# Moving the ring of low weight parts by 64 bytes in SBUF

## What is computed

```
first_block, per layer:   h = x @ w_in;  three attention branches;  gates * (branch @ w_branch)
                          x = layernorm(ALPHA*x + merged @ w_out)
                          x = layernorm(ALPHA*x + square(relu(x @ mlp_w1)) @ mlp_w2)
second_block, per layer:  u = rmsnorm(h);  u @ w_in_2;  SSD, HGRN2 and mLSTM branches
                          h += merged @ w_out_2
                          h += (silu(conv(u @ w_up)) * v) @ w_down
                          h += (p @ w_ple) * sigmoid(h @ w_ple_gate)
out = rmsnorm(h)
```

## Time and profile before

| | |
|---|---|
| time, median of 3 runs | 2486.16 us (2485.28 to 2489.66) |
| the profiled execution's own time | 2493.97 us |
| its span, first to last instruction | 2492.2 us |
| mean granted TensorE clock | 0.994 |
| PE busy, PEld busy | 98%, 90% of the span |
| DVE, ACT, POOL busy | 72%, 58%, 12% of the span |

### The profile page before, as it was taken

The page is one execution under the profiler, slowest core; times in us unless marked ns, Lnnn a source line. Parts: engine busy times, 40 slices in busy tenths (PEclk is TensorE's granted clock), DMA queues, the critical chain, the costliest instruction groups (busy, mean ns, idle before and its releaser), DMA issues.

```text
span 2492.2 us, 43110 instructions
## 1 busy us (share of the span) xinstructions
PE 2440.8 (98%) x17744; PEld 2232.4 (90%) x17744; DVE 1786.6 (72%) x2889; ACT 1452.0 (58%) x2130; POOL 291.6 (12%) x222
## 2 busy tenths in 40 slices
PE   8999999999999999899999999999999999999998
PEld 8888999988889899799999799998898999899996
DVE  4567675565576755669867887885599768887875
ACT  5547555445466455467665655664667656656654
POOL 0000002000000000002222720000012207500000
PEclk9999999999999999899999999999999999999999
DMA  7554476555544565555566655566554567645663
GB/s 248 157 145 118 154 247 193 186 185 168 140 125 142 173 201 186 168 158 144 145 178 186 194 153 192 187 192 197 149 161 135 162 191 197 184 148 190 189 210 127
DMA packets 358920, 430.50 MB, mean 173 GB/s; under 512 B 20616, under 2 KB 286310, under 8 KB 358468
## 3 DMA queue, kind: packets, MB, share of 16 engines
q1 hardware_dynamic: 341312, 401.72, 53.1%
q10 hardware_dynamic: 14340, 14.93, 2.7%
q0 software_dynamic: 3072, 11.10, 1.5%
HBM read 424.44 MB, written 3.24 MB: 172 GB/s over the span
## 4 chain that ended last, share of the span: by engine, by line
PE 87%; DVE 9%; ACT 2%; issue 1%; DMA 1%; ACTq 0%; POOL 0%; POOLq 0%; DVEq 0%
PE ps L112 85%; PE ps L115 2%; DVE wlo L121 2%; DVE sE L121 1%; DVE hgA L148 1%; DVE hgQF L121 0%; DVE hgQB L121 0%; ACT lnv L118 0%; DVE hgkf L121 0%; DVE hgkb L121 0%; DMA kT<-in_diff_lambda 0%; DVE sbc L130 0%; DVE sE L124 0%; DMA memN<-in_mem 0%; DVE hgTf L121 0%
## 5 line engine op out<-in xcount | busy, mean ns | idle before, releaser
L121 DVE TENSOR_TENSOR wlo<-wring,whi 128x1024 fp32r<-128x1024 f32 (+1 forms) x768 | 919.2, 1217 | 252.7 <-ACT whi L118 252.1
L118 ACT ACTIVATE whi<-wring 128x1024 fp32r<-128x1024 f32 (+1 forms) x768 | 803.5, 1054 | 427.9 <-PE ps L112 415.8
L112 PE MATMUL ps<-uT,whi 128*128 128x256 f32 x4640 | 817.8, 280 | 6.1 <-DVE wlo L121 4.5
L112 PEld LDWEIGHTS ps<-uT,whi 128*128 128x128 f32 x4640 | 705.8, 188 | 16.4 <-DVE wlo L121 7.5
L112 PE MATMUL ps<-uT,wlo 128*128 128x256 f32 x2320 | 645.4, 278 | 0.0
L112 PEld LDWEIGHTS ps<-uT,wlo 128*128 128x128 f32 x2320 | 436.1, 188 | 0.0
L112 PE MATMUL ps<-xT,whi 128*128 128x256 f32 x2112 | 381.0, 284 | 2.9 <-DVE xT L121 1.7
L112 PEld LDWEIGHTS ps<-xT,whi 128*128 128x128 f32 x2112 | 323.4, 188 | 9.7 <-issue 5.6
L112 PE MATMUL ps<-xT,wlo 128*128 128x256 f32 x1056 | 296.4, 281 | 0.0
L112 PE MATMUL ps<-whi,hid 128*128 128x512 f32 x864 | 270.4, 392 | 0.0
L112 PEld LDWEIGHTS ps<-xT,wlo 128*128 128x128 f32 x1056 | 199.4, 189 | 0.3
(11 more groups left out here) (400 smaller groups left out, 3576.9 us busy)
## 6 DMA issues: line engine op xcount, KB each, us to landing
wring<-in_w_in SPq DMA_DIRECT2D x346, 512.0 KB, 4.2
wring<-in_mlp_w SPq DMA_DIRECT2D x128, 512.0 KB, 4.4
wring<-in_w_up SPq DMA_DIRECT2D x88, 512.0 KB, 4.5
wring<-in_w_down SPq DMA_DIRECT2D x44, 512.0 KB, 4.5
wring<-in_w_branch SPq DMA_DIRECT2D x32, 512.0 KB, 3.4
wring<-in_w_out SPq DMA_DIRECT2D x32, 512.0 KB, 4.6
wring<-in_mem_w_kv SPq DMA_DIRECT2D x16, 512.0 KB, 5.9
wring<-in_w_br_hg SPq DMA_DIRECT2D x16, 512.0 KB, 4.6
```

The source lines that it names most:

```text
L112: return self.e.matmul(*p, **k) if self.e else Nothing()
L118: return self.e.activation(*p, **k) if self.e else Nothing()
L121: return self.e.tensor_tensor(*p, **k) if self.e else Nothing()
```

## The change

The tensor of the low parts gets 32 floats (128 bytes) more, and the ring is the stretch of it that begins 16 floats (64 bytes) in. So all operands from `wlo` begin at 64 modulo 128. `wring` and `whi` stay where they are. Everything allocated behind `wlo` moves by 128 bytes, so its place modulo 128 stays, the arena's too; the arena's size, rounded down to 64 floats, stays 36672 floats, and so does every offset in it.

```
-    K.whi, K.wlo = sb("whi", NS * WN, F32R), sb("wlo", NS * WN, F32R)
+    K.whi, K.wlo = sb("whi", NS * WN, F32R), sb("wlo", NS * WN + 32, F32R)[:, 16:16 + NS * WN]
```

## The result

The changed kernel takes 2532.84 us (median of 4 runs, 2525.15 to 2533.62); the kernel before, run beside it, 2486.8 us (2485.28 to 2489.66). The ratio is 1.0168, 95% interval 1.0146 to 1.0189: 1.7% slower. The forecast was 2500 us with a range up to 2520, so the direction held and the size did not: 42 us by the ratio (0.0168 x 2486.8), 46 us by the two medians, where 14 were forecast. The profiled execution took 2533.62 us, its span 2531.8 us. Beside the traced execution of before, itself a slow one of its kernel (2493.97 us where the median is 2486.8), the span grew by 2531.8 - 2492.2 = 39.6 us.

A forecast was written before the change was run, and what follows sets the result against it. TensorE's matmul pace was taken to bound the kernel. Features +13.6 us and tokens +2.1 us, times 0.9, gave +14 us on the 2486.2 us median: 2500 us, range 2464 to 2520.

The forecast's parts named there:

- What bounds the kernel: TensorE, busy 98% of the span, sets the time; features triples have two steady speeds, 13.5 ns apart.
- Its signs: Features' wlo groups at 279 ns or more, none at 276, no triple at 0.340 us; uneven steps; token groups leaving 389.
- VectorE, 0: The subtraction's output shifted by 64 bytes costs 1 ns, 0.8 us over 768, mostly beside TensorE's work; taken as 0.
- A wait or an engine that becomes late: No wait is added; VectorE, if slowed, would be late on the 9% of the chain that is DVE.
- The features' term: One odd load in three costs 1950 quick features triples 7 ns each: +13.6 us, bounds -26.6 and +26.3.
- The tokens' terms: Token triples with stationary operand at 0: 304 x 7 ns = +2.1 us; about 780 at 64: 0, bounds -6.8 and +8.8.
- The upper end of the range: Range top 2520 us, above 2517 us for all features slow and tokens at their bound, less a tenth.
- The tenth taken off: Features before a wait on wlo or a transposition gain nothing, so the summed TensorE terms were multiplied by 0.9.
- The move of everything else by 128 bytes, 0: Everything behind wlo moves by 128 bytes but keeps its place modulo 128; cost taken as 0.
- third rival: With a 256-byte pattern, the arena's move changes activations' distance to whi; all features slow, +26.3, about 2514 us; chance 8%.
- First rival, likeness helps: Load and stream at the same place modulo 128 run faster on TensorE: 2477 us, down to 2453; chance 36%.
- Second, places don't matter: Features' two speeds come from how work falls after each break, not place: 2486 us, give or take 4; chance 16%.

The follow-up runs named there:

- both64: Kernel before with both rings (high and low parts) beginning at 64 modulo 128, arena where it was: 2535.61 us, ratio 1.0173.
- x0all: Kernel before with the whole arena beginning 64 bytes further on, rings unmoved, most activations at distance 0 from both rings: 2539.25 us, ratio 1.0214.
- lo128: Kernel before with the low ring alone moved by 128 bytes modulo 256, constants allocated between the rings: 2484.99 us, ratio 0.9976.
- pad128: Kernel before with only what lies behind the low ring moved by 128 bytes, the ring staying at 0 modulo 128: 2524.13 us, ratio 1.013.
- w256: Kernel before with a 256-byte buffer allocated ahead of the rings instead of behind, moving both rings by 256 bytes, arena unmoved: 2483.32 us, ratio 1.0.
- (192, 64): Placement of lo128 and best: activations start 192 bytes past the high ring and 64 past the low ring, modulo 256; ratios 0.9976 and 0.9977.
- (192, 192): Placement of the kernel before and w256: most activations start 192 bytes past both rings, modulo 256; ratios 1 and 1.0.
- best: lo128 with three buffers (first-block merged, second-block hid, hT) 64 bytes lower: 2483.01 us, ratio 0.9977 to the kernel before.
- x160: Kernel before with the rings beginning 32 bytes further on, arena unmoved: 2532.24 us, ratio 1.0185.
- x224: Kernel before with the arena beginning 32 bytes further on, rings unmoved: 2535.01 us, ratio 1.0197.
- pad_lo128: lo128 with `wlo` 32 floats longer, moving everything behind the rings by 128 bytes: 2506.34 us, ratio 1.0074 to the kernel before.
- before_xl64: Kernel before with the low halves of uT alone 64 bytes further on, rings untouched: 2507.11 us, ratio 1.0078.

## Why the prediction was wrong

**What bounds the kernel** was read rightly: TensorE's pace, with two steady speeds of features at 340 and 353.5 ns, and the place of operands modulo some power of two behind it. The 40 us between the traces are of that kind. Its signs came true as well: the wlo groups of features have 283 and 282 ns, 16 quick triples are left, the steps are uneven, and the token groups at 389 rose.

**VectorE, 0:** right, 1222 ns. **A wait or an engine that becomes late:** none.

**The features' term is the step that failed.** The prediction said that a triple with one odd step "cannot settle in the same way", and the quick speed did go, but then it took for it "the nearest measured cost of an operand at the other place, 7 ns a triple". If the quick speed can't be reached, the quick triples fall all the way to the slow speed, which the same profile had at 13.5 ns. Measured: 16 quick triples left, and a mean of 353.2 where it was 346.0. The term was 13.6 us and came out at 28 us by paces; the bound of +26.3 stood in the text, and was the value that the argument called for. The count was a little off as well: by starts 56% of triples were quick before, about 2200 and not 1950, since I had read it from mean durations. The reason given, that "both steady speeds stand on three equal steps", was not right either, and that the quick speed went is in part luck: both64 and x0all have three equal steps and no quick speed, and lo128 has one step of three at another distance than the others and the most quick triples of all. The prediction had named this as its weak point, "a period-three pattern that fits the quick speed better than equal steps do".

**The tokens' terms** failed in the same way, and were too small. At 0: 7 ns a triple for one odd step, 12.4 measured, 3.8 us for 2.1. At 64: I took 0, "between gain by likeness and loss by unevenness", and measured 11.8 ns, 9.2 us; that is near my upper bound of 8.8. It was the second largest term and I had set it at nothing.

**The upper end of the range** did not hold the prediction's own bounds. All features slow and tokens at their bound was given as 2517 us; with both token bounds it is (26.3 + 6.1 + 8.8) x 0.9 = 37 us, 2523.

**The tenth taken off** for matmuls behind waits was too much: 41 us by paces are 39.6 in the span, 4% less.

**The move of everything else by 128 bytes, 0:** wrong. pad128 shows 1.3% for it alone. My third rival had this with a chance of 8% and a price of 28 us; the trace did not exclude it and I gave it too little. Its "all features slow" is nearly so (352.0 ns, 340 quick triples left), and tokens lose 9 and 17 ns. In the changed kernel it is not a term that adds to the other, but each of the two is enough.

**First rival, likeness helps:** wrong for features (359.2 ns at distance 0), right for tokens when all steps are alike (681 to 684). With one step of three alike, as in the change itself, neither gains: 353.2 and 702.3 ns.

**Second, places don't matter:** wrong, though what it said of the two speeds is half true: inside a placement that allows the quick speed, the speed is settled anew between stretches, and before and w256, placed alike, differ in which stretches find it (xT: 336 quick of 986, and 751 of 991). The rule cited from the Trainium skill, page "SBUF — State Buffer", section "SBUF: two separate sides", says that engine ports other than VectorE's and GpSimd's shared pair never wait on anyone. It would give no difference; before and x0all differ by 2.1% with nothing changed but where the arena begins. The measurement decides. That it is a wait at a port is not shown, though.

Not settled: what has the length of 256 bytes, whether the quick speed goes with the distance or with the places modulo 128 themselves, why (192, 64) finds the quick speed so much more often than (192, 192), and whether a matmul's own operands or successive streams are the pair that counts.

## What to carry to other kernels

Where float32r matmuls run back to back, the start addresses of stationary and moving operands are a tuning knob, worth over 2% from the worst to the best here (x0all and best), that costs no instruction to turn; sweep them in steps of 64 bytes over 256, each ring by itself, for products with 256 and with 512 columns separately, and keep in mind that a pad anywhere ahead moves everything behind it. When a steady speed rests on a pattern that one changed step can break, price the break at the whole distance to the next speed, not at the share of the steps changed. Read the pace from starts, not from durations.

## What the runs showed of the hardware

- A triple of 256-column float32r matmuls takes 340 ns at its quick speed and 352 to 360 otherwise; of 512 columns 681 to 703. Both depend on where the operands begin: moving what lies behind the rings by 128 bytes costs 1.3% (pad128), moving the rings by 256 bytes changes nothing (w256: 1.0, 0.9986 to 1.0013).
- 32 bytes off cost as much as 64 (x160, x224: no quick triple of 3735 and 3733).
- The quick speed, once found, lasts to the end of the run of like matmuls: of the 81 long runs of each kernel none goes back once three triples are quick, in before, w256, lo128, best, pad_lo128, pad128 or before_xl64. Which speed the next run has is settled anew. The fastest placement makes the quick one the rule (90% of the triples).
- Halving VectorE's and ScalarE's busy time by leaving out most of the splitting changed no pace of TensorE by more than 2 ns a triple (346.0 and 344.9 in features, 690.5 and 688.7 in tokens).
